# Expert weights dealt to the partitions in runs of consecutive rows, with the token rows and activations read in the matching strided order

## The reference, cut to what matters

```
h   = rms_norm(x, norm2_w)                       # the gain norm2_w is per channel
hid = silu(h_e @ w_gate[e]) * (h_e @ w_up[e])    # w_gate, w_up: [32, 1024, 512]
y_e = hid @ w_down[e]                            # w_down: [32, 512, 1024]
x   = x + sum over the token's two experts of weight * y_e
```

## Time and profile before

| | us |
|---|---|
| median of 3 runs | 1738.31 (1730.54 to 1743.97) |
| span of the profiled execution | 1736.7 |
| PE matmul busy | 1530.3 (88% of the span) |
| PE weight load busy | 1111.7 (64%) |
| DVE busy | 938.1 (54%) |
| ACT busy | 732.4 (42%) |
| POOL busy | 206.5 (12%) |

### The profile page before, as it was taken

One profiled execution on the slowest core, in us unless ns is written; L12 is line 12 of the kernel. 1 busy time (PEld: TensorE's weight loads), 2 busy tenths in 40 slices (PEclk: granted clock), 3 DMA queues, 4 the chain that ended last, 5 costly groups with the idle time before them and its releaser, 6 DMA issues.

```text
span 1736.7 us, 19764 instructions
## 1 busy us (share of the span) xinstructions
PE 1530.3 (88%) x6777; PEld 1111.7 (64%) x6778; DVE 938.1 (54%) x1073; ACT 732.4 (42%) x847; POOL 206.5 (12%) x260
## 2 busy tenths in 40 slices
PE   7899977795499999999999995998889999969959
PEld 6788744444366776667667763544368788858846
DVE  6733154305288788888887883073454324421543
ACT  4432223202187787787787871142033212331130
POOL 1011000104312111111111110031000000000030
PEclk8999767797699999999999996997979999989979
DMA  5222600112299999999999995400002122241301
GB/s 196 92 74 77 231 11 1 53 49 97 72 349 357 364 347 358 362 349 358 357 358 363 347 319 185 161 5 25 0 29 96 69 97 97 97 145 49 121 6 43
DMA packets 135508, 293.91 MB, mean 169 GB/s; under 512 B 18222, under 2 KB 20380, under 8 KB 135452
## 3 DMA queue, kind: packets, MB, share of 16 engines
q1 hardware_dynamic: 122812, 270.64, 43.6%
q10 hardware_dynamic: 7024, 14.06, 2.2%
q0 software_dynamic: 5616, 8.44, 1.6%
HBM read 289.15 MB, written 12.88 MB: 174 GB/s over the span
## 4 chain that ended last, share of the span: by engine, by line
PE 61%; ACT 17%; DVE 10%; issue 6%; DMA 2%; ACTq 2%; POOL 1%; SPq 0%; DVEq 0%; POOLq 0%
ACT hi L1291 13%; PE ps L791 10%; PE ps L812 9%; PE ps L458 7%; PE ps L618 5%; PE ps L626 4%; PE ps L570 3%; PE ps L765 3%; PE ps L844 3%; PE ps L605 2%; PE ps L413 2%; PE ps L672 2%; PE ps L502 2%; PE ps L537 1%; DVE M L1734 1%
## 5 line engine op out<-in xcount | busy, mean ns | idle before, releaser
L1728 DVE TENSOR_TENSOR ring_r<-ring,hi 128x2048 fp32r<-128x2048 f32 x192 | 426.7, 2289 | 1.3 <-issue 1.3
L1291 ACT ACTIVATE hi<-ring 128x2048 fp32r<-128x2048 f32 x192 | 355.9, 1903 | 0.0
L1470 DVE TENSOR_TENSOR ring_r<-ring,ring_r 128x4096 fp32r<-128x4096 f32 x25 | 110.6, 4425 | 175.2 <-ACT ring_r L1162 175.2
L812 PE MATMUL ps<-ring_r,ats 128*128 128x512 f32 x768 | 179.0, 396 | 4.0 <-DVE ats L1865 3.2
L812 PEld LDWEIGHTS ps<-ring_r,ats 128*128 128x128 f32 x768 | 147.2, 192 | 35.9 <-issue 4.8
L1162 ACT ACTIVATE ring_r<-ring 128x4096 fp32r<-128x4096 f32 x25 | 90.5, 3620 | 168.3 <-PE ps L812 133.7
L618 PE MATMUL ps<-hi,XTS 128*128 128x512 f32 x512 | 129.0, 395 | 4.5 <-DVE XTS L1739 2.6
L1018 POOL TENSOR_TENSOR rsv<-msv,half 128x1 f32<-128x1 f32 (+2 forms) x32 | 32.9, 1031 | 839.1 <-DVE msv L1430 839.0
L618 PE MATMUL ps<-ring_r,XTS 128*128 128x512 f32 x512 | 131.1, 398 | 0.8 <-issue 0.8
L649 PE MATMUL ps<-hi,HIDS 128*64 128x512 f32 x512 | 129.2, 394 | 0.0
L791 PE MATMUL ps<-ring_r,ring_r 128*128 128x512 f32 x512 | 123.2, 393 | 1.9 <-DVE hi L1853 1.9
(11 more groups left out here) (286 smaller groups left out, 1960.2 us busy)
## 6 DMA issues: line engine op xcount, KB each, us to landing
ring<-in_w_gate SPq DMA_DIRECT2D x32, 2048.0 KB, 10.0
ring<-in_w_up SPq DMA_DIRECT2D x32, 2048.0 KB, 10.7
ring<-in_w_down SPq DMA_DIRECT2D x32, 2048.0 KB, 7.9
ring<-in_w_ff SPq DMA_DIRECT2D x16, 2048.0 KB, 8.2
ring<-in_w_in SPq DMA_DIRECT2D x8, 2048.0 KB, 8.7
X<-in_x ACTq DMA_DIRECT2D x8, 512.0 KB, 5.0
ring<-in_w_out SPq DMA_DIRECT2D x2, 2048.0 KB, 7.9
M<-results ACTq DMA_DIRECT2D x8, 512.0 KB, 7.4
```

The source lines that it names most:

```text
L812: ins = pe.matmul(ps[:, 2 * t + c, :], ATS[a][:, 4 * (n % 4) + k, t * P:(t + 1) * P], w[b][:, k, c * 512:(c + 1) * 512], start=(n % 4 == 0 ...
L1291: act.activation(HI[u][:, c], ring[:, s, c], ACT.Copy).then_inc(w_hi, 1)
L1470: vec.tensor_tensor(ring_r[s][:, :], ring[:, s, :], split_hi[j % 2][:, :].bitcast(F32), ALU.subtract).then_inc(s_lo, 1)
L1728: vec.tensor_tensor(ring_r[s][:, c], ring[:, s, c], HI[u][:, c].bitcast(F32), ALU.subtract).then_inc(w_lo, 1)
```

## The change

Row p*8 + k of w_gate and w_up (p*4 + k of w_down) now goes to partition p as its k-th piece: a partition gets one run of 16 KB per weight. Channel p*8 + k of a token then has to lie on partition p as well, so `turn_rows` takes every eighth column of XG from column k on; hidden column p*4 + f has to lie on partition p for the down product, so `summed` takes every fourth column of GUS. The gains norm2_w are needed in the same dealing: a new DMA on the ACT queue brings them to the new tile GAIN2, ahead of the loads of the router's biases, and DVE waits for it once before the first `rows_gained`.

```diff
+        GAIN2 = m(15360, DT)
...
+        gain2_in = sem("gain2_in")
...
@@ turn_rows
                     ins = pe.matmul(ps[:, 6 + a, k * 2 * BLK:(k + 1) * 2 * BLK],
-                                    XG[:, (4 * a + k) * P:(4 * a + k + 1) * P], SUM2[0:BLK, :], start=True, stop=True)
+                                    XG.rearrange("b (p k) -> b k p", k=DT)[:, 4 * a + k, :], SUM2[0:BLK, :],
+                                    start=True, stop=True)
@@ summed
-                        ins = pe.matmul(ps[:, 2 + u, f * P:(f + 1) * P], GUS[:, u, f * P:(f + 1) * P], SUM2,
+                        ins = pe.matmul(ps[:, 2 + u, f * P:(f + 1) * P], GUS[:, u, :].rearrange("r (p f) -> r f p", f=FT)[:, f, :], SUM2,
                                         start=True, stop=True)
@@ load_expert
-                    src = A[w][0, bass.ds(e, 1)].rearrange("e (k p) c -> p (e k) c", p=P)
+                    src = A[w][0, bass.ds(e, 1)].rearrange("e (p k) c -> p (e k) c", p=P)
@@ ACT queue, after the final_out of the mixer
             small(WR[:, :, NG:NG + NE], A["w_expert"][0].rearrange("(k p) c -> p k c", p=P), router_in)
+            small(GAIN2, A["norm2_w"][0].rearrange("(p k) -> p k", k=DT), gain2_in)
             small(BR[:, 0:NG], A["b_group"].to_broadcast([P, NG]), router_in)
@@ DVE
-            gain = prm[:, R_N2:R_N2 + DT].rearrange("p (a k) -> p a k", a=2).unsqueeze(3).to_broadcast([P, 2, 4, BLK])
+            gain = GAIN2.rearrange("p (a k) -> p a k", a=2).unsqueeze(3).to_broadcast([P, 2, 4, BLK])
...
             vec.wait_ge(consts2, N_CONSTS2)
+            vec.wait_ge(gain2_in, 16)
             rows_gained(0)
```

## The result

The changed kernel is slower: 1889.53 us (median of 4 runs, 1884.3 to 1890.05) against 1737.87 for the kernel before in the same comparison; ratio 1.0865, 95% interval 1.0839 to 1.0891. That is 152 us more, where 99 were forecast, and above the range's end of 1860. The profiled execution has a span of 1888.0 us. (In the changed kernel's numbering L605 is L607, L618 is L621, L626 is L629, L649 is L652, L1291 is L1295, L1734 is L1738, L1744 is L1748.)

A forecast was written before the change was run, and what follows sets the result against it. The prediction took a loop through ACT, PE and DVE in the expert stage as the bound; stepped PE loads add 3.08 us in each of 32 blocks, 99 us, all else 0, giving 1837 us, range 1730 to 1860 us.

The forecast's parts named there:

- What bounds the kernel: Expert stage: a loop through ACT, PE and DVE sets the 18.4 us per expert; weight loads have 10.8 us of slack.
- Rival 3: Expert stage: 16 KB runs lower the DMA rate until loads set the period; 1799 us without PE penalty; chance 0.04.
- rival 4: Expert stage: something waits unseen for loads and PE has no penalty; at most 32 us faster, 1706 us; chance 0.03.
- GAIN2 and the relief of DVE and ACT: The extra gains DMA is hidden, and fewer weight packets give DVE and ACT nothing back: 0 for both.
- The stepped reads as the cause: PE's reads of XG (32 B steps) and GUS (16 B steps) make the whole loss, 99 us.
- Rival 1: PE's loads do not care for the step: 111 ns a load stay, 1738 us; chance 0.20.
- rival 2: Only the 32 B step in L605 costs, the 16 B step in L626 is free: 46 us, 1784 us; chance 0.05.
- The price of a stepped load: Each stepped PE load in L605 and L626 costs +102 ns, or 0.82 us per group of eight.
- The DVE pair: DVE reductions L1718 (contiguous, 286 ns) and L1683 (32 B step, 377 ns), carried over to price PE's stepped loads.
- PE does not become a second bound: Expert stage: PE's load grows by 3.28 to 20.6 us, below the new period of 21.4 to 21.5 us.
- DMA share 0.84: Expert stage: the DMA engines' busy share falls from 0.98 to about 0.84 as the period lengthens.

The follow-up runs named there:

- run 1: Changed kernel with XG and GUS read contiguously again, keeping the 16 KB weight runs and GAIN2: 1742.41 us, ratio 1.0008.
- run 2: Changed kernel with the stepped reads of XG and GUS, but weights loaded in the 2 and 4 KB runs of before: 1884.76 us, ratio 1.0835.
- run 4: Changed kernel with only the 16 B step in GUS, XG read contiguously: 1807.97 us, ratio 1.0394.
- run 3: Changed kernel with only the 32 B step in XG, GUS read contiguously: 1795.73 us, ratio 1.0323.
- run 7: Changed kernel with PE's reads contiguous; DVE (normed rows) and ACT (copy out of PSUM) do the reordering instead: 1743.48 us, ratio 1.0013.
- run 9: Changed kernel with the first half of the row turning moved ahead of summed(0): 1915.60 us, ratio 1.1014.
- run 5: Changed kernel with XG and GUS read contiguously and each product of the four groups done twice: 1847.72 us, ratio 1.0623.
- run 6: Changed kernel with other steps: 12 and 24 B in XG's halves, 8 and 12 B in GUS for gate and up: 1805.45 us, ratio 1.0375.
- run 8: Kernel before, with the first half of the row turning moved ahead of summed(0): 1734.03 us, ratio 0.9963.

## Why the prediction was wrong, step by step

**What bounds the kernel: right.** The reading that the expert stage with its DMA share of 0.98 is set by a loop over ACT, PE and DVE, and not by the loads, is shown by run 1: 8 % less work for the DMA engines, ratio 1.0008. Rival 3 (the DMA becomes the bound) and rival 4 (faster) fall with it.

**GAIN2 and the relief of DVE and ACT: right, at 0.** L1728 has 2286 ns after, 2289 before.

**The stepped reads as the cause: right.** Runs 1 and 2 put the whole loss on them. Rival 1 is refuted, and so is rival 2: run 4 shows the 16 B step to cost 1.94 us an expert at the full clock.

**The price of a stepped load: too low.** This is the first step that failed. The DVE pair gave +91 ns read as an added cost and +113 read as a rate, and I took the middle, +102. Measured is 231 to 234 ns in place of 111, +120 to +123. The argument in my own text, that 1.75 ns a column looks like a limit of the memory side, asked for the reading as a rate, and that came nearer: 1.8 ns a line on PE, 1.75 on DVE. Averaging it with a reading that I had argued against threw 11 ns away, and the rest lay outside both. A group so grew by 1.0 to 1.1 us instead of 0.82, and by runs 3 and 4 the loop by 3.82 us an expert instead of 3.08. That is 0.74 x 32 = 24 us. How near the DVE row came was in part luck: in run 7 DVE reads by the same 32 B step at 1.13 ns a column at most, so 1.75 is not what the step costs DVE everywhere, and no run shows one limit behind both figures.

**"PE does not become a second bound": wrong.** This is the second step. I added 3.28 us to PE's 17.4 at the full clock and compared the sum with the loop. I did not ask what the slow loads do to the clock. At the full clock the step would have held: the experts of run 9 that keep 1.00 have both steps, and PE is busy for 21.30 us of their 22.08 and waits for ACT. In the changed kernel the granted clock falls within the second of the three adjacent groups, the first L652 products take 3.67 us instead of 2.0, PE is busy all the time, and the mean period of 23.03 us exceeds the loop's 22.19. That is 0.84 x 32 = 27 us. With the two corrections the sum is 1837 + 24 + 27 = 1888 us; measured were 1889.5. The corrections are taken from the runs, so this sum tests only that they add up. The expectation of DMA share 0.84 failed for the same reasons: the period was longer, and the engines needed less for the same bytes (0.71).

**What stays open.** That stepped loads, and not the length of the groups, precede the lower clock is shown by runs 5 and 6: three contiguous groups of 1.98 us keep it in every expert, three stepped ones of 1.6, 1.6 and 2.1 us lose it in every expert. What exactly the clock reacts to is not shown, and the order of the groups does not decide it alone. It falls in all experts of the changed kernel and of run 6, in every second one of run 9, in three of 28 of run 4, whose stepped groups stand singly, and in none of run 3; no run tells what differs between two experts that do the same work. The Trainium skill ("TensorE: Matmul & The Clock Gate", Part 1) ties the lower level to a PE that has been idle. In this trace PE counts as busy 184.00 us in 184 at a clock of 0.87; so the busy time of the profile does not show the idleness meant there, if it is that. In run 8, where every load is contiguous, the profile does show idleness before the fall: PE's wait of 3.1 us. The 0.84 us is a difference of means; a changed kernel in its own order of groups with the clock held at 1.00 was not among the runs.

## What to carry to other kernels

If the source of a layout change is a transfer that nobody waits for, its gain is nothing, and the price is in the reads that must match it: look for the operand whose innermost step grows, above all PE's stationary one. Put such a step where an engine reads it for nothing or reads it once (here ACT out of PSUM, and four tiles on DVE), not into a load that is repeated a thousand times. And when PE's small groups get slower, add the clock to the sum: a PE that is always busy in the profile can still lose it. Read single periods before a mean: in runs 4, 8 and 9 the mean stood for two kinds of expert, and for neither.

## What the runs showed of the hardware

- PE's load of 128 fp32 columns from SBUF is spaced 111 ns contiguous, 135 at 8 B, 174 at 12 B, 220 to 234 from 16 B on.
- The granted clock goes to its lower level for some microseconds from within adjacent groups of such loads on, with PE busy throughout. In the changed kernel (three groups in a row) it does so in every expert and L652 pays, 394 to 507 ns in the mean; with two and two groups (run 9) in every second expert; with single groups in three of 28 (run 4) or none (run 3).
- Weights in 16 KB runs are one packet each and take the DMA engines 0.90 of the time at 354 GB/s, against 0.98 at 356 GB/s for 2 and 4 KB runs; 512 floats out of PSUM in 16 B steps take ACT 588 ns, as contiguous ones do.
- DVE's normed rows (1024 floats) take 753 ns read contiguously and 1152 ns by a step of 32 B.
